# The samples' top-k search moved from VectorE to ScalarE, and masks, own rows and turned rows reordered, in a hybrid decoder step

## The reference, cut to what matters

```python
gq, gk, gv, glr, gr, dq, dk, dv, iq, ik, iw = split_columns(h @ w_in)
# GLA, chunk by chunk
new_state = exp(b_last)[..., None] * state + einsum('bhsk,bhsv->bhkv', k * exp(b_last - b), v)
# DSA: a cheap indexer scores all positions, the best 256 are attended to
sc = einsum('bths,bth->bts', relu(iq . ik * IDX_DIM ** -0.5), iw * IDX_HEADS ** -0.5)
sc = where(kpos <= qpos, sc, -inf)
_, idx = lax.top_k(sc, 256)              # rows of up to 1024 (prompt) and 1028 (samples) positions
s = where(valid, q . k_sel * HEAD_DIM ** -0.5, -inf);  p = softmax(s);  o = p . v_sel
```

## Time and profile before

| | us |
|---|---|
| median of 3 runs (1251.54 to 1253.86) | 1252.87 |
| profiled execution | 1255.62 |
| its span, first to last instruction | 1253.9 |
| PE busy | 1083.3 (86%) |
| DVE busy | 652.3 (52%) |
| ScalarE (ACT) busy | 346.2 (28%) |
| GpSimd (POOL) busy | 127.2 (10%) |
| mean granted PE clock | 0.915 of full speed |

### The profile page before, as it was taken

How to read it: one execution, slowest core, us unless ns; L and a number is a source line. 1 busy time by engine, 2 the same in 40 slices (tenths; PEclk the granted TensorE clock), 3 DMA queues, 4 the chain that set the end, 5 groups by cost and what they waited for, 6 DMA issues and landing times. The chain is left out here.

```text
span 1253.9 us, 15126 instructions
## 1 busy us (share of the span) xinstructions
PE 1083.3 (86%) x4998; PEld 521.6 (42%) x4998; DVE 652.3 (52%) x1360; ACT 346.2 (28%) x754; POOL 127.2 (10%) x205
## 2 busy tenths in 40 slices
PE   3899999979799996976899999995699999999910
PEld 2594433324354544443444445554333333333300
DVE  3300589999899992973666513335212222222239
ACT  5221652100123322143677611112111111111113
POOL 0302000000000002322000000000201111111041
PEclk9799999989899996986999999996699999999965
DMA  9412514530400003243400101113797875576456
GB/s 350 177 43 52 201 34 170 203 137 0 97 5 1 1 1 105 68 135 119 98 1 1 35 33 67 67 55 122 274 366 285 320 278 192 206 269 253 180 205 243
DMA packets 70485, 170.82 MB, mean 136 GB/s; under 512 B 25511, under 2 KB 39959, under 8 KB 60041
## 3 DMA queue, kind: packets, MB, share of 16 engines
q1 hardware_dynamic: 55916, 122.77, 27.8%
q0 software_dynamic: 14496, 47.12, 10.5%
HBM read 237.18 MB, written 23.91 MB: 208 GB/s over the span
## 5 line engine op out<-in xcount | busy, mean ns | idle before, releaser
L963 PE MATMUL psum<-mem 128*128 128x512 f32 (+4 forms) x544 | 166.4, 465 | 13.3 <-DMA mem<-in_w_in 7.9
L1422 PE MATMUL psum<-mem 128*64 128x512 f32 x768 | 172.8, 603 | 3.9 <-DMA mem<-in_w_exp_up 2.8
L986 PE MATMUL psum<-mem 128*128 128x512 f32 x320 | 140.9, 596 | 0.0
L963 PEld LDWEIGHTS psum<-mem 128*128 128x128 f32 (+1 forms) x544 | 93.4, 193 | 80.7 <-issue 75.1
L1346 PE MATMUL psum<-mem 128*128 128x512 f32 x256 | 111.1, 592 | 0.6 <-issue 0.6
L1950 DVE TENSOR_SCALAR_CACHE_REDUCE marks<-mem,top_try_low 128x384 uint16<-128x384 uint16 (+6 forms) x112 | 104.0, 993 | 0.6
L1950 DVE TENSOR_SCALAR_CACHE_REDUCE marks<-mem,top_try 128x384 bf16<-128x384 bf16 (+6 forms) x105 | 97.5, 993 | 0.5
L1422 PEld LDWEIGHTS psum<-mem 128*64 128x64 f32 x768 | 53.9, 139 | 105.1 <-issue 100.9
L986 PEld LDWEIGHTS psum<-mem 128*128 128x128 f32 x320 | 59.9, 190 | 79.4 <-issue 75.2
L1446 PE MATMUL psum<-mem 128*64 128x512 f32 x384 | 89.3, 608 | 2.4 <-DVE mem L2323 2.4
L2331 DVE TENSOR_TENSOR mem<-psum,mem 128x256 f32<-128x256 f32 x24 | 10.2, 425 | 150.1 <-ACT mem L1806 150.1
(11 more groups left out here) (374 smaller groups left out, 1355.0 us busy)
## 6 DMA issues: line engine op xcount, KB each, us to landing
mem<-in_w_exp_gate SPq DMA_DIRECT2D x48, 1024.0 KB
mem<-in_w_exp_up SPq DMA_DIRECT2D x48, 1024.0 KB
mem<-in_w_exp_down SPq DMA_DIRECT2D x48, 1024.0 KB
mem<-in_w_ada SPq DMA_DIRECT2D x24, 1024.0 KB, 9.2
y_of_slot<-mem POOLq DMA_DIRECT2D x24, 512.0 KB, 4.1
mem<-in_x_prompt SPq DMA_DIRECT2D x16, 512.0 KB, 4.8
mem<-in_w_in SPq DMA_DIRECT2D x3, 2048.0 KB, 7.9
h_rows<-mem POOLq DMA_DIRECT2D x8, 512.0 KB, 2.9
```

Of the source, the lines that this page charges most:

```text
L963: mm = pe.matmul(bank[0:rows(i), to:to + width], h_t[:, k, cols(i)], w[:, k, c0:c0 + width], start=(k == 0), stop=(k == KT - 1))
L986: mm = pe.matmul(bank[:, 0:n_t], w[:, k, c0:c0 + P], h_t[:, k, t0:t0 + n_t], start=(k == 0), stop=(k == KT - 1))
L1422: mm = pe.matmul(psum[half_rows(half), 2 + u, :].rearrange("p (n f) -> p n f", n=2), x_slot_t[:, u, k, half_rows(half)], gate_up_w[2 * u + ...
```

## The change

Four edits. (1) The samples' row set leaves DVE's counts. ScalarE does its search with the sign function: a scan with a sum, the sign of the sum against a bound, and a step of the shift, each waiting for the one before. The 15 high bits stand among the keeps of gq/gk, seven low bits behind the keeps of gv2 to gv8, two in GLA chunk 0 and one in each of chunks 1 to 7. The low search starts on a key that DVE gives after its joins. (2) The adaln slices are spread over 10 gqk jobs and not 13. (3) k_own moves from POOL to DVE, which then makes the cuts and the first three masks ahead of the samples' state. (4) PE adds the samples' mask and makes their scores ahead of `turn_mix_g`; ScalarE's keeps are interleaved with the two exponentials.

```diff
@@ PE
-                for n_pass, k in slices[j * len(slices) // n_gqk:(j + 1) * len(slices) // n_gqk]:
+                for n_pass, k in slices[j * len(slices) // (n_gqk - 3):(j + 1) * len(slices) // (n_gqk - 3)]:
...
                     pe.wait_ge(s_attn_masked, TILES)
                     pe.wait_ge(s_gla_k_kept, TILES)
+                    pe.wait_ge(s_k_own, 1)
...
             pe.wait_ge(s_k_seq_t, NSEQ)
-            for i in range(TILES):
-                turn_mix_g(i)
-
             pe.wait_ge(s_masks, NT - 1)
-            pe.wait_ge(s_mix_g_t, TILES)
             for half in range(2):
...
+            for i in range(TILES):
+                turn_mix_g(i)
+            pe.wait_ge(s_mix_g_t, TILES)
@@ ScalarE
+            samp_keys = (samp_halves.bitcast(mybir.dt.int16), samp_halves)
+            def samp_bit(phase, i):
+                n_bits = (HIGH_BITS, LOW_BITS)[phase]
+                if i == 0:
+                    act.wait_ge(s_samp_key, phase + 1)
+                    if phase == 0:
+                        act.wait_ge(s_out_a, 16 * 6)
+                own.wait(own.did(act.activation(samp_marks, samp_keys[phase], ACT.Sign, bias=samp_shift[:, 0:1], accum_out=samp_signs[:, 0:1])))
+                own.wait(own.did(act.activation(samp_keep[:, :], samp_signs[:, :], ACT.Sign, bias=samp_bound[:, 0:1])))
+                if i + 1 < n_bits:
+                    own.wait(own.did(act.activation(samp_shift[:, :], samp_keep[:, :], ACT.Identity, scale=-2.0 ** (n_bits - 2 - i),
+                                                    bias=samp_shift[:, 0:1])))
+                else:
+                    own.wait(own.did(act.activation(samp_keep[:, :], samp_keep[:, :], copy, scale=0.5)))
+                    act.activation(samp_found[:, :], samp_shift[:, :], ACT.Identity, scale=-1.0, bias=samp_keep[:, 0:1]).then_inc(s_samp_found, 1)
...
             for n in range(first_gqk, first_gqk + 5):
                 keep(n)
+                if n >= first_gqk + 2:
+                    samp_bit(*next(samp_next))
...
             for n in range(first_gqk + 5, first_gqk + 7):
                 keep(n)
+                samp_bit(*next(samp_next))
...
             for n in range(first_gqk + 7, first_gv + 1):
                 keep(n)
+                if n < first_gv:
+                    for _ in range(1 if jobs[n][2] == 2 else 2):
+                        samp_bit(*next(samp_next))
             keep_ada(2, ada_m1)
             for n in range(first_gv + 1, first_gr):
                 keep(n)
+                if n >= first_gr - 7:
+                    samp_bit(*next(samp_next))
...
                 if c >= 1:
                     rstd_gla(c - 1)
+                if c < NT:
+                    for _ in range(2 if c == 0 else 1):
+                        samp_bit(*next(samp_next))
...
-            for i in range(TILES):
-                keep_mix_g(i)
             for half in range(2):
+                for i in range(3 * half, 3 * half + 3):
+                    keep_mix_g(i)
                 act.wait_ge(s_samp_min, half + 1)
...
+            for i in range(6, TILES):
+                keep_mix_g(i)
@@ SP and POOL, ahead of the far key pages
             sp.wait_ge(s_top, TOP_STEPS)
+            sp.wait_ge(s_samp_found, 2)
@@ POOL
-            pool.wait_ge(s_gla_k_kept, TILES)
-            for b in range(NSEQ):
-                last = pool.tensor_scalar(k_own[:, b, :], ...)
             last.then_inc(s_own_rows, 1)
@@ DVE
-                for j, (i, r, width) in enumerate(rowsets):
+                for j, (i, r, width) in enumerate(rowsets[:n_tiles]):
...
+            own.did(dve.tensor_scalar(samp_bound[:, :], top_want[0:NS, n_tiles:n_sets], -2.0, float(LS + 1), ALU.mult, ALU.add))
+            own.did(dve.memset(samp_shift[:, :], 0.5 - 2.0 ** (HIGH_BITS - 1)))
+            own.wait()
+            dve.sem_inc(s_samp_key, 1)
...
             for j, (i, r, width) in enumerate(rowsets):
+                if j == n_tiles:
+                    dve.wait_ge(s_samp_found, 1)
+                    own.did(dve.tensor_scalar(top_t[0:NS, j:j + 1], samp_found[:, :], 65536.0, None, ALU.mult))
+                    own.did(dve.memset(samp_shift[:, :], 0.5 - 2.0 ** (LOW_BITS - 1)))
+                    own.wait()
                 ...
                 joined.append(own.did(dve.tensor_tensor(low[j], low[j], mark, ALU.add)))
+            own.wait()
+            dve.sem_inc(s_samp_key, 1)
...
+            MASKS_FIRST = 3
             for c in range(TILES):
                 ...
                 else:
                     (mask of the samples' logits, as before)
+                    dve.wait_ge(s_gla_k_kept, TILES)
+                    for b in range(NSEQ):
+                        last = dve.tensor_scalar(k_own[:, b, :], k_rows[0:NS, NT % 2, :, :].rearrange("p j c -> p (j c)"),
+                                                 K("seq_row", NS)[:, b:b + 1], None, ALU.mult)
+                    last.then_inc(s_k_own, 1)
+                    find_cuts()
+                    for j in range(MASKS_FIRST):
+                        make_mask(j)
...
             mix_gla(TILES - 1)
+            for j in range(MASKS_FIRST, n_sets):
+                make_mask(j)
```

More of the change, by code:

```diff
@@ L424, in hybrid_decoder_step @@
         top_cut = sb("top_cut", [P, 7])
+        samp_shift = sb("samp_shift", [NS, 1])
+        samp_signs = sb("samp_signs", [NS, 1])
+        samp_keep = sb("samp_keep", [NS, 1])
+        samp_bound = sb("samp_bound", [NS, 1])
+        samp_found = sb("samp_found", [NS, 1])
         p_min = sb("p_min", [P, 4])
@@ L790, in _ @@
                 for j in range(2):
-                    pool.tensor_copy(q_own[at_half, :, j, half * DT:(half + 1) * DT],
-                                     gq_t[at_half, j, SEQ:TOK].rearrange("p (b t) -> p b t", t=DT))
-            pool.wait_ge(s_gla_k_kept, TILES)
-            for b in range(NSEQ):
-                last = pool.tensor_scalar(k_own[:, b, :], k_rows[0:NS, NT % 2, :, :].rearrange("p j c -> p (j c)"),
-                                          K("seq_row", NS)[:, b:b + 1], None, ALU.mult)
+                    last = pool.tensor_copy(q_own[at_half, :, j, half * DT:(half + 1) * DT],
+                                            gq_t[at_half, j, SEQ:TOK].rearrange("p (b t) -> p b t", t=DT))
             last.then_inc(s_own_rows, 1)
@@ L1602, in _ @@
             first_gv = job_of["gv", 0, 0]
+            samp_at = sum(P * (i + 1) for i in range(2, NT))
+            samp_halves = halves[0:NS, samp_at:samp_at + LS]
+            samp_keys = (samp_halves.bitcast(mybir.dt.int16), samp_halves)
+            samp_marks = at(KS + 6528, LS // 2, r=NS).bitcast(BF16)
+            def samp_bit(phase, i):
[12 more added lines that the diff above has]
+                    act.activation(samp_found[:, :], samp_shift[:, :], ACT.Identity, scale=-1.0, bias=samp_keep[:, 0:1]).then_inc(s_samp_found, 1)
+            samp_bits = [(phase, i) for phase, n_bits in enumerate((HIGH_BITS, LOW_BITS)) for i in range(n_bits)]
+            samp_next = iter(samp_bits)
             for n in range(first_gla, first_gqk):
@@ L1664, in _ @@
                     rstd_gla(c - 1)
+                if c < NT:
+                    for _ in range(2 if c == 0 else 1):
+                        samp_bit(*next(samp_next))
             rstd_gla(TILES - 1)
+            assert next(samp_next, None) is None
             act.wait_ge(s_own_rows, 1)
@@ L2055, in mix_gla, with find_cuts, make_mask @@
                 last.then_inc(s_mix_g, 1)
+            def find_cuts():
+                dve.wait_ge(s_top, TOP_STEPS)
+                own.did(dve.tensor_copy(top_try[:, :], top_low[:, :]))
+                own.wait()
+                dve.wait_ge(s_samp_found, 2)
+                own.did(dve.tensor_copy(top_try[0:NS, n_tiles:n_sets], samp_found[:, :]))
+                own.wait()
+                own.did(dve.tensor_tensor(top_t[:, :], top_t[:, :], top_try[:, :], ALU.bitwise_or))
+                own.wait()
+                own.did(dve.tensor_scalar(top_keep_f[:, :], top_t[:, :].bitcast(F32), 2.0 ** -126, None, ALU.is_ge))
+                own.wait()
+                own.did(dve.tensor_tensor(top_cut[:, :], top_t[:, :].bitcast(F32), top_keep_f[:, :], ALU.mult))
+                own.wait()
+                own.did(dve.tensor_tensor(top_cut[:, :], top_cut[:, :], top_sign[:, :], ALU.mult))
+                for j, (i, r, width) in enumerate(rowsets):
+                    own.did(dve.tensor_scalar(score[i][0:r, 0:width], score[i][0:r, 0:width], top_sign[0:r, j:j + 1], None, ALU.mult))
+                own.wait()
+                count_above([top_cut[0:r, j:j + 1] for j, (i, r, width) in enumerate(rowsets)], ALU.is_gt)
+                own.wait()
+                own.did(dve.tensor_scalar(top_want[:, :], top_count[:, :], -1.0, float(TOPK), ALU.mult, ALU.add))
+            def make_mask(j):
+                i, r, width = rowsets[j]
+                x, cut = score[i][0:r, 0:width], top_cut[0:r, j:j + 1]
```

(18 more changed lines are left out.)

25 lines of the change are left out of this document (15 added, 10 removed).

## The result

| | before, us | after, us |
|---|---|---|
| median | 1253.3 (1251.54 to 1253.86, 4 runs) | 1240.6 (1239.81 to 1241.29, 4 runs) |
| ratio to before | | 0.9891 (95%: 0.9868 to 0.9913) |
| profiled execution; its span | 1255.62; 1253.9 | 1239.81; 1238.1 |
| mean granted PE clock | 0.915 | 0.926 |
| PE, DVE, ScalarE, POOL busy | 1083.3, 652.3, 346.2, 127.2 | 1073.4, 617.0, 401.3, 121.8 |

The account below looks back on a forecast made before the run. PE bounds it, held by DVE and gv weights until GLA, the POOL-DVE-ScalarE order at chunk 8, then masks. Terms -6.6 and -6.6 give -13.2 on 1255.62: 1242.4, less 2.75 to the median: 1240, range 1236 to 1243.

Parts of the forecast that it names:

- the two old ones: PE's idle up to 345 us before the change: 7.92 us for gv weights, 8.05 us for DVE's gk.
- some 10 us faster: Gv stretch: sign of a wrong forecast, if ScalarE had no wait behind gv2; total then some 10 us faster.
- The rival of dearer bits: ScalarE's search: Sign needs its own table, 1.28 us per load; 1242 to 1245 us; chance 0.12.
- the bounds: ScalarE's one-column step: between 0.1 and 0.4 us, the upper beside a copy of 0.36; 0.28 taken.
- The cost taken for the fall: GLA loop at O3: PE's clock falls after a 2.9 us wait, costing 4.9 us.
- Rival 1: PE's clock stays up after O3's wait, chunk 8 or both: 1228 to 1235 us; chance 0.24.
- The last term: Last key scores to first prompt scores: 21.0 us instead of 27.6, a gain of 6.6.
- the 0.9 us for exponentials among the keeps: Scores before mix turns: ScalarE's exponentials standing among its keeps add 0.9 us to that stretch.
- what follows 572 us is untouched: After the first prompt scores: later work is unchanged and started by events, so no further gain was counted.
- The slower rival: ScalarE's wait for the second key delays gv5; loss if key later than 321; +8, 1261 us; chance 0.07.
- the swallowed gains: Rival: unseen waits, such as key pages or value pages, take the gains back; 1248 to 1253 us; chance 0.09.

Follow-up runs that it names:

- Better versions: Changed kernel with ScalarE's low bits all in GLA chunks and DVE's low bits respread, 1210.62 us; the same with chunk 8 reordered on DVE and ScalarE, 1210.27 us.
- The last experiment: Against the 1210.62 us kernel with respread DVE low bits: DVE's mask ahead of mix_gla(6), ScalarE's copy of inter ahead of the Silu table; 1210.27 us.
- the split alone: Kernel before, with only q_own and k_own (still on POOL) given a semaphore each: 1251.12 us, ratio 0.9985.

## Why the prediction was right, point by point

**The gv stretch.** Right in mechanism and size. Forecast: key at 307.8, PE idle 292.2 to 310.4, GLA at 333.6, O0 at 342.2. Measured: 308.1, 18.91 us up to 310.68, 334.02, 342.57. That this wait replaces the two old ones is shown from both sides: without it 20.7 us are won, and with the weights' wait put back nothing changes. The forecast said "some 10 us faster" without it; it is 20.7, as gk was ready in time.

**A bit on ScalarE.** 1.9 us forecast, 1.95 measured, the last 2.13 (474.69 to 476.82) against 2.2. The rival of dearer bits falls. (The copy of 0.36 us that the bounds name is 32x256 in the earlier trace rows, not 128x256; nothing hangs on it.) ScalarE's timeline over the end of the search:

```profile
473.19 1.28 ACT L1676 ACT_TABLE_LOAD   x1
474.48 0.30 ACT L1676 ACTIVATE mem<-mem,const 128x4 f32<-128x4 f32 x1
474.69 1.16 ACT L1621 ACTIVATE mem<-mem,samp_shift 32x1056 bf16<-32x1056 uint16 x1
...
476.53 0.29 ACT L1628 ACTIVATE samp_found<-samp_shift,samp_keep 32x1 f32<-32x1 f32 x1
476.73 0.36 ACT L1683 ACTIVATE mem<-psum 32x256 f32<-32x256 f32 x1
477.10 1.28 ACT L1547 ACT_TABLE_LOAD   x1
478.40 0.59 ACT L1547 ACTIVATE mem<-psum 32x512 f32<-32x512 f32 x1
478.89 0.57 ACT L1691 ACTIVATE mem<-psum 128x512 f32<-128x512 f32 x1
```

The scan follows the square root with no load between them. The Trainium skill ("ScalarE: Activation LUTs", "Rules for kernel authors") advises VectorE rather than ScalarE for relu, max, min, add and mul, up to about three times faster in bf16. The prediction stretched this to a scan with a sum, which is none of them, and the trace shows no such advantage: the scan takes 1.16 us here and 1.30 to the next step, DVE's bf16 count 1.30 and 1.34.

**Chunks 0 to 3.** O3 at 382.6 with 2.9 us of wait and a fall of the clock was forecast; it is 383.19, 2.97 us and 0.61. The cost taken for the fall, 4.9 us, is 4.7 in the pair of profiles under "Better versions". Rival 1 (clock kept) fell here and at chunk 8. For chunk 4 on -0.7 was forecast; O4 is at 407.30 and was at 407.62, -0.3.

**Chunk 8.** 479.5 forecast, 479.61 measured, by ScalarE's chain as described (the rows above). One step failed without a price: PE's idle for the mask was 3.06 us and not 0.9. I had left out that mix_gla(6), ahead of DVE's mask, waits for ScalarE's square root, whose table load is the 473.19 row. DVE's timeline:

```profile
474.81 0.18 DVE L2105 RECIPROCAL mem<-mem 128x4 f32<-128x4 f32 x1 [2.10 <-ACT mem L1676]
...
476.08 0.27 DVE L2169 TENSOR_TENSOR mem<-psum,const 32x128 f32<-32x128 f32 x1
477.12 2.18 DVE L2174 TENSOR_SCALAR mem<-mem,const 32x256 f32<-32x256 f32 x8 [0.77 <-ACT mem L1683]
```

It was harmless, since the copy of inter ends later. The last experiment took this wait away and had DVE's bits in its place. DVE's k_own took 2.18 us and not 2.7. Two parts of the 6.5 us were tried apart: the split alone gave 3.0 in its profile, with PE 3.9 us late there, and k_own left on POOL costs 1.62 us of wait, 2.9 by the medians, whose intervals overlap. They don't add up to 6.5, and what the split gives with PE in time was not measured.

**Masks and scores.** 538.4 was forecast with the masks there since 534.2, and 538.40 is measured with no wait; DVE's last mask ended at 533.5. The last term was mis-sized: 21.0 us were forecast to the prompt's scores, and it took 22.8. The part that failed is the 0.9 us for exponentials among the keeps: the nine turned rows with the table load in them were to take 8.7 us (6.5 + 1.3 + 0.9) and took 11.4. In the window 545 to 556 PE is busy 7.03 of 11 us and waits for keeps that stand behind the exponentials, and the clock is 0.66, which the term left out. Against this stands a gain that "what follows 572 us is untouched" denied: the prompt's first two score groups ran at 1.99 and 2.86 us, not 3.78, and 2.8 us more are won by 589.25 (-14.3 instead of -11.5). The two misses, +1.8 and -2.8, nearly cancel, and that is luck.

**The sum.** By the profiles -13.2 was forecast, -15.8 measured. The last 1.5 us of it lie in PE's last products with the down-projection weights of the experts. PE's timeline of before, then of after:

```profile
1193.40 5.35 PE L1446 MATMUL psum<-mem 128*64 128x512 f32 x16 [2.36 <-DVE mem L2323]
```
```profile
1179.41 3.65 PE L1452 MATMUL psum<-mem 128*64 128x512 f32 x16 [2.36 <-DVE mem L2396]
```

They start 14.0 us earlier, and behind the same wait they took 5.35 us at a granted clock of 0.68 in the one execution and 3.65 at 1.00 in the other. No edit touches them, so this difference is of the two executions and hardly of the change, and the forecast gets no credit for it. By the medians it is -12.7, which my figure of 1240 met partly by luck: it took off 2.75 us because the profiled execution of before lay above its median, while that of after lies 0.8 below its own. The slower rival (key later than 321) fell with the key at 308.1, and so did the swallowed gains: no page load released PE between 479 and 561.

## What to carry to other kernels

An item put into an in-order list costs what its wait holds behind it, not what it runs: 1.95 us of work behind the keep of gv2 cost 20.7. When one late event ends several waits, removing the early ones only lengthens the last; look for the event, and place what waits for it behind everything that doesn't. Where several producers share a semaphore, ask for each reader which one it needs; and count a reordering with the clock its products will run at: of two orders of the same work here the shorter one brought PE to the prompt's scores at the low clock, and the medians don't tell them apart.

## What the runs showed of the hardware

- The sign function needed no table load in any of 31 bits, whether the exponential's, Silu's or the square root's table was in. A table load takes 1.28 us and the next function starts 0.01 to 0.02 us behind it.
- A chain of one-column steps on ScalarE costs 0.29 us a step plus 0.03 for its own wait.
- POOL's eight 32x256 products took 9.21 us with DVE busy beside them and 7.84 in before, DVE's 2.18; and DVE's seven scalings took 4.56 us beside POOL instead of 3.73 in after. DVE's timeline with k_own on POOL:

```profile
476.98 4.56 DVE L2134 TENSOR_SCALAR mem<-mem,top_sign 128x384 f32<-128x384 f32 x7
```

- PE's clock fell in one profile behind a wait of 0.46 us among the O products and stayed up in another behind 0.47, as it had in before behind 0.95. Behind the waits of 1.75 to 3 us at O2 or O3 it fell in every profile taken here (granted 0.50 to 0.68 in the window behind them). One such fall cost 4.7 us from O3 to O4.
